# Mixture-of-experts decoder step: the down projection of an expert's first token block multiplied one expert later

## What is computed

```python
def swiglu(x, w_gate, w_up, w_down):
    return (jax.nn.silu(x @ w_gate) * (x @ w_up)) @ w_down
...
        xb = x_pad[tok]
        yb = swiglu(xb, w_gate[e], w_up[e], w_down[e]) * w[:, None]
        return acc.at[tok].add(yb), None
```

## Time and profile before

| | |
|---|---|
| Median of 3 runs | 1901.25 us (1900.89 to 1901.89) |
| Profiled execution, its own time | 1903.72 us |
| Span of its instructions | 1901.9 us |
| Mean granted clock of TensorE in it | 0.962 |
| TensorE busy over the span | 1716.1 us (90%) |
| VectorE, ScalarE, GpSimd busy | 968.8, 779.8, 513.7 us |

### The profile page before, as it was taken

The page is one execution under the profiler, slowest core; times in us unless marked ns, Lnnn a source line. Parts: engine busy times, 40 slices in busy tenths (PEclk is TensorE's granted clock), DMA queues, the critical chain, the costliest instruction groups (busy, mean ns, idle before and its releaser), DMA issues. The chain is left out here.

```text
span 1901.9 us, 25091 instructions
## 1 busy us (share of the span) xinstructions
PE 1716.1 (90%) x7154; PEld 1075.3 (57%) x7155; DVE 968.8 (51%) x1639; ACT 779.8 (41%) x1453; POOL 513.7 (27%) x733
## 2 busy tenths in 40 slices
PE   6999999978985699999999998999999999937998
PEld 4666666545774456556656655656665565623443
DVE  3333333314996354555444545445555544637885
ACT  2222222212331355665555555545556554721221
POOL 0000110000665332333332334223333322411221
PEclk9999999987998799999999998999999999978999
DMA  9200000021111787888777768767787776958650
GB/s 360 100 0 0 0 0 0 15 96 47 67 67 62 255 294 257 274 286 292 255 243 248 257 232 299 246 228 271 260 280 274 260 253 222 337 219 331 270 166 28
DMA packets 124013, 363.70 MB, mean 191 GB/s; under 512 B 28966, under 2 KB 44262, under 8 KB 121389
## 3 DMA queue, kind: packets, MB, share of 16 engines
q1 hardware_dynamic: 87909, 290.85, 44.2%
q0 software_dynamic: 35760, 72.49, 10.7%
q10 hardware_dynamic: 320, 0.07, 0.0%
HBM read 334.52 MB, written 71.91 MB: 214 GB/s over the span
## 5 line engine op out<-in xcount | busy, mean ns | idle before, releaser
L1409 PE MATMUL Y<-raw_d,hT 128*128 128x512 f32 (+1 forms) x768 | 352.1, 602 | 19.7 <-ACT hT L1469 19.7
L197 DVE TENSOR_TENSOR lo_gu<-raw_g,hi_gu 128x1024 fp32r<-128x1024 f32 x130 | 153.5, 1221 | 366.5 <-ACT hi_gu L190 321.3
L1367 PE MATMUL GU<-hi_gu,x_hi 128*128 128x512 f32 (+1 forms) x768 | 322.0, 419 | 5.7 <-issue 4.1
L1367 PE MATMUL GU<-hi_gu,x_lo 128*128 128x512 f32 (+1 forms) x768 | 304.6, 397 | 0.0
L1367 PE MATMUL GU<-lo_gu,x_hi 128*128 128x512 f32 (+1 forms) x768 | 304.3, 396 | 0.0
L1477 ACT ACTIVATE y<-Y,w_t 128x512 f32<-128x512 f32 (+1 forms) x256 | 168.3, 683 | 238.5 <-PE Y L1409 230.6
L1328 POOL DMA_INDIRECT y_dram<-y,to_row x128 | 131.3, 1026 | 472.0 <-ACT y L1477 354.0
L1409 PEld LDWEIGHTS Y<-raw_d,hT 128*128 128x128 f32 (+1 forms) x768 | 132.3, 179 | 178.7 <-issue 167.3
L1317 POOL DMA_INDIRECT rows<-rows_dram,from_row x131 | 159.0, 1214 | 109.1 <-POOL from_row L1315 76.8
L1367 PEld LDWEIGHTS GU<-hi_gu,x_hi 128*128 128x128 f32 (+1 forms) x768 | 136.8, 178 | 77.4 <-issue 39.6
L107 POOL TENSOR_SCALAR st<-st 128x1 f32<-128x1 f32 (+3 forms) x45 | 14.4, 321 | 582.5 <-ACT junk L585 201.0
(11 more groups left out here) (221 smaller groups left out, 2139.3 us busy)
## 6 DMA issues: line engine op xcount, KB each, us to landing
raw_g<-in_w_exp_gate SPq DMA_DIRECT2D x130, 512.0 KB, 5.9
raw_u<-in_w_exp_up SPq DMA_DIRECT2D x130, 512.0 KB, 6.2
raw_d<-in_w_exp_down SPq DMA_DIRECT2D x130, 512.0 KB, 4.9
yk<-y_dram SPq DMA_DIRECT2D x16, 2048.0 KB, 12.7
rows_dram<-row SPq DMA_DIRECT2D x9, 512.0 KB, 2.7
h_dram<-resid SPq DMA_DIRECT2D x9, 512.0 KB, 2.7
w_big<-in_w_in SPq DMA_DIRECT2D x2, 2048.0 KB, 12.8
w_out<-in_w_out SPq DMA_DIRECT2D x1, 4096.0 KB, 18.1
```

The source lines that it names most:

```text
L197: dve.tensor_tensor(part_of(keep, "lo", m, par, h), part_of(keep, "raw", m, par, h), part_of(keep, "hi", m, par, h).bitcast(F32), ALU.subt ...
L1367: ins = pe.matmul(out, lhs[x], rhs[w], start=first and i == 0, stop=last and i == 2)
L1409: ins = pe.matmul(Y[half][0:n, :], hT[b][:, f, :], raw_d[par][:, f, cols], start=f == 0, stop=f == FC - 1)
```

## The change

On TensorE `down(0, ...)` of an expert no longer stands in its own turn but in that of the next expert, with the other `raw_d` buffer (`1 - par`) and a second `hT` buffer. In `one_block` its half 0 stands between the transposes and `h_transposes(0)`, half 1 after that. In `two_blocks` the first matmul of half 0 stands before `h_transposes(0)`, the second between `gate_up(1)` and `h_transposes(1)`, half 1 where it was; `down(1, ...)` stays with its own expert. The first turn multiplies zeros, and one `down(0, ...)` with its copies and its scatter follows the loop. The tables `to_t`, `idx_t` and `w_t` have a column more in front, so that block 0 finds the entry of the expert before.

On SP `load` asks for `gate` and `up` of the next expert (`following`) as before, and last for `down` of this turn's expert `e`, when the first of the counts of the turn before is there. TensorE waits for it before half 1. The first `down` weights are no longer loaded at the start of the router but at the start of the expert stage, where SP waits for them.

```diff
@@ -142,9 +142,9 @@
-                    to_t=mid("to_t", [P, 2, PAIRS + 2], I32),
-                    idx_t=mid("idx_t", [P, 2, PAIRS + 2], I32),
-                    w_t=mid("w_t", [P, 2, PAIRS]),
+                    to_t=mid("to_t", [P, 2, PAIRS + 3], I32),
+                    idx_t=mid("idx_t", [P, 2, PAIRS + 3], I32),
+                    w_t=mid("w_t", [P, 2, PAIRS + 1]),
@@ -915,8 +915,6 @@ (router, SP)
-            for h in range(2):
-                sp.dma_start(part_of(keep, "raw", "d", 0, h), expert_weights(a, "d", 0, h)).then_inc(keep[f"d_ld{h}"], 16)
@@ -1191,7 +1189,9 @@
 
 
             own.did(dve.memset(keep["fill"][:, E:PAIRS], CAP))
-            own.did(dve.memset(keep["to_t"][:, :, PAIRS:PAIRS + 2], Y_ROWS))
+            own.did(dve.memset(keep["to_t"][:, :, 0:1], Y_ROWS))
+            own.did(dve.memset(keep["to_t"][:, :, PAIRS + 1:PAIRS + 3], Y_ROWS))
+            own.did(dve.memset(keep["w_t"][:, :, 0:1], 0.0))
             dve.wait_ge(count_done, TILES + 1)
             own.did(dve.tensor_copy(count[:], C[0:1, 0:E]))
             own.wait()
@@ -1205,11 +1205,11 @@
             own.did(dve.tensor_scalar(rounds[:], top[:, 1:2], 1.0, None, ALU.add))
             dve.wait_ge(tab_ld, 32)
             for b in range(2):
-                own.did(dve.tensor_copy(keep["to_t"][:, b, 0:PAIRS], tab[:, b, :, 0]))
+                own.did(dve.tensor_copy(keep["to_t"][:, b, 1:PAIRS + 1], tab[:, b, :, 0]))
             own.wait()
             own.did(dve.tensor_scalar(keep["idx_t"][:], keep["to_t"][:], 3, None, ALU.logical_shift_right))
             for b in range(2):
-                own.did(dve.tensor_copy(keep["w_t"][:, b, :], tab[:, b, :, 1]))
+                own.did(dve.tensor_copy(keep["w_t"][:, b, 1:PAIRS + 1], tab[:, b, :, 1]))
             own.wait()
 
 
@@ -1229,7 +1229,7 @@
         hi_gu, lo_gu, raw_d = (keep[n] for n in ("hi_gu", "lo_gu", "raw_d"))
         x_hi = [sb(f"x_hi{b}", [P, KC, BLK[b]], F32R) for b in range(2)]
         x_lo = [sb(f"x_lo{b}", [P, KC, BLK[b]], F32R) for b in range(2)]
-        hT = [sb(f"hT{b}", [P, FC, BLK[b]]) for b in range(2)]
+        hT = [[sb(f"hT0{i}", [P, FC, P]) for i in range(2)], [sb("hT1", [P, FC, BLK[1]])] * 2]
         rows = [sb(f"rows{b}", [P, D]) for b in range(2)]
         y = [sb(f"y{b}", [P, D]) for b in range(2)]
         sig = [sb(f"sig{b}", [P, FE]) for b in range(2)]
@@ -1271,17 +1271,17 @@
                              (ple[0:NS, SAMPLE, :], a["p_sample"][0].rearrange("b s d -> (b s) d"))):
                 sp.dma_start(dst, src).then_inc(keep["output_ld"], 16)
 
-            def load(e, m, par):
+            def load(e, following, m, par):
 
                 for name in "gu":
                     for h in range(2):
                         sp.wait_ge(lo_set[name], 2 * m + h + 1)
-                        sp.dma_start(part_of(keep, "raw", name, 0, h), expert_weights(a, name, e, h)).then_inc(
+                        sp.dma_start(part_of(keep, "raw", name, 0, h), expert_weights(a, name, following, h)).then_inc(
                             ld[name][h], 16)
 
+                sp.wait_ge(y_done[1], 2 * m + 1)
                 for h in range(2):
-                    sp.wait_ge(y_done[1], 2 * m + 1)
-                    sp.dma_start(part_of(keep, "raw", "d", 1 - par, h), expert_weights(a, "d", e, h)).then_inc(
+                    sp.dma_start(part_of(keep, "raw", "d", par, h), expert_weights(a, "d", e, h)).then_inc(
                         ld["d"][h], 16)
 
             def gate(n):
@@ -1289,16 +1289,20 @@
                 sp.dma_start(keep["w_big"][:, bass.ds(at, GATE_PIECE)], gate_w[:, bass.ds(at, GATE_PIECE)]).then_inc(
                     gate_ld, 16)
 
-            sp.sem_inc(y_done[1], 1)
+            for h in range(2):
+                sp.dma_start(part_of(keep, "raw", "d", 1, h), expert_weights(a, "d", 0, h)).then_inc(ld["d"][h], 16)
+            for h in range(2):
+                sp.wait_ge(ld["d"][h], 16)
+            sp.sem_inc(y_done[1], 2)
             n_rounds = sp.value_load(rounds[0:1, 0:1], min_val=1, max_val=ROUNDS)
             with sp.Fori(0, n_rounds) as r:
                 with sp.Fori(0, E // 2 - 1) as i:
                     for par in range(2):
-                        e = sp.snap(2 * i + par + 1)
-                        load(e, r * E + 2 * i + par, par)
+                        following = sp.snap(2 * i + par + 1)
+                        load(sp.snap(2 * i + par), following, r * E + 2 * i + par, par)
                         gate(2 * i + par)
                 for n in (E - 2, E - 1):
-                    load((n + 1) % E, r * E + n, n % 2)
+                    load(n, (n + 1) % E, r * E + n, n % 2)
                     gate(n)
                 sp.wait_ge(gate_ld, 16 * E * r + 16 * E)
                 sp.sem_inc(sp_passed, 1)
@@ -1312,7 +1316,7 @@
 
             def gather(b, m):
                 n = BLK[b]
-                own.did(pool.tensor_copy(from_row[b][0:n, :], idx_t[0:n, b, bass.ds(m, 1)]))
+                own.did(pool.tensor_copy(from_row[b][0:n, :], idx_t[0:n, b, bass.ds(m + 1, 1)]))
                 own.wait()
                 pool.indirect_dma_start(
                     out=rows[b][0:n, :], out_offset=None, in_=rows_dram[:, :],
@@ -1322,7 +1326,7 @@
             def scatter(b, m):
                 n = BLK[b]
                 pool_after(pool, keep["passed"], y_st[b], 16 * m + 16)
-                own.did(pool.tensor_copy(to_row[b][0:n, :], to_t[0:n, b, bass.ds(m, 1)]))
+                own.did(pool.tensor_copy(to_row[b][0:n, :], to_t[0:n, b, bass.ds(m + b, 1)]))
                 own.wait()
                 pool_after(pool, keep["passed"], y_ev[1], 2 * m + b + 2)
                 pool.indirect_dma_start(
@@ -1355,9 +1359,11 @@
             own.clear()
             each_pair(pool, pair)
             n = pool.value_load(rounds[0:1, 0:1], min_val=1, max_val=ROUNDS)
+            scatter(0, pool.snap(n * E))
+            own.clear()
             for b in range(2):
                 pool_after(pool, keep["passed"], rows_ld[b], n * (16 * E) + (32 if b == 0 else 16))
-                pool_after(pool, keep["passed"], y_st[b], n * (16 * E) + 16)
+                pool_after(pool, keep["passed"], y_st[b], n * (16 * E) + (32 if b == 0 else 16))
 
         @block.tensor
         def _(pe):
@@ -1398,26 +1404,32 @@
                     ins = pe.transpose(GU[b][:, f * n:(f + 1) * n], hid[b][0:n, f * P:(f + 1) * P], ident[0:n, 0:n])
                 ins.then_inc(h_tr[b], 1)
 
-            def down(b, m, par, half, counts):
+            def down(b, m, par, half, counts, fs=range(FC), more=True):
+
                 n = BLK[b]
-                pe.wait_ge(h_ev[b], m + 2)
-                pe.wait_ge(y_ev[half], 2 * m + b + 1)
                 cols = slice(half * 512, (half + 1) * 512)
-                for f in range(FC):
+                if fs[0] == 0:
+                    pe.wait_ge(h_ev[b], m + b + 1)
+                    pe.wait_ge(y_ev[half], 2 * m + b + 1)
+                for f in fs:
                     if b == 0 and half == 0:
                         pe.wait_ge(ld["d"][f], 16 * m + 16)
-                    ins = pe.matmul(Y[half][0:n, :], hT[b][:, f, :], raw_d[par][:, f, cols], start=f == 0, stop=f == FC - 1)
-                ins.then_inc(y_done[half], counts)
+                    if b == 0 and half == 1 and more:
+                        pe.wait_ge(ld["d"][f], 16 * m + 32)
+                    ins = pe.matmul(Y[half][0:n, :], hT[b][par][:, f, :], raw_d[par][:, f, cols], start=f == 0, stop=f == FC - 1)
+                if fs[-1] == FC - 1:
+                    ins.then_inc(y_done[half], counts)
 
             def two_blocks(m, par):
                 gate_up(0, m, par)
                 transposes(1, m)
                 transposes(0, m + 1)
+                down(0, m, 1 - par, 0, 1, (0,))
                 h_transposes(0, m)
                 gate_up(1, m, par)
-                down(0, m, par, 0, 1)
+                down(0, m, 1 - par, 0, 1, (1,))
                 h_transposes(1, m)
-                down(0, m, par, 1, 1)
+                down(0, m, 1 - par, 1, 1)
                 down(1, m, par, 0, 1)
                 down(1, m, par, 1, 1)
 
@@ -1428,9 +1440,9 @@
                 pe.sem_inc(h_tr[1], 1)
                 gate_up(0, m, par)
                 transposes(0, m + 1)
+                down(0, m, 1 - par, 0, 2)
                 h_transposes(0, m)
-                down(0, m, par, 0, 2)
-                down(0, m, par, 1, 2)
+                down(0, m, 1 - par, 1, 2)
 
             def pair(m, par):
                 filled = pe.value_load(keep["fill"][0:1, bass.ds(m, 1)], min_val=0, max_val=SEQ + NS)
@@ -1439,9 +1451,12 @@
                 with pe.If(filled < P + 1):
                     one_block(m, par)
 
-            pe.wait_ge(blank, 3)
+            pe.wait_ge(blank, 4)
             transposes(0, 0)
             each_pair(pe, pair)
+            m = pe.value_load(rounds[0:1, 0:1], min_val=1, max_val=ROUNDS) * E
```

(20 more changed lines are left out.)

## The result

The changed kernel takes 1915.38 us (median of 6 runs, 1910.35 to 1919.16) where the kernel before, on the same chip, takes 1901.07: a ratio of 1.0074, interval 1.0065 to 1.0084. It is slower by 0.7%; the forecast was 1891, faster by 0.5%. The profiled execution took 1915.49 us (span 1913.6), 11.8 more than that of before.

A forecast was written before the change was run, and what follows sets the result against it. TensorE, busy 995 of 1049 us, was taken to bound the expert stage. Terms -45.1 + 22.4 + 10.7 + 3.5 - 2 = -10.5 us took the profiled 1903.72 to 1893.2, as a median 1891; 8-in-10 range 1876 to 1902.

The forecast's parts named there:

- Removed waits: TensorE's waits for hid (25.4 us) and hT (19.7 us) in the expert stage all go: -45.1 us.
- The added wait in two-block turns: TensorE stands before the second block's h_transposes, with only 2 records ahead: 0.70 us per turn, 32 turns, +22.4 us.
- the lower bound: The added two-block wait counted as idle in a busy table, not by starts: 0.54 us per turn, 17.3 us.
- Lead given up by ScalarE and VectorE: In runs of one-block turns these engines' 11.37 us loop lags the faster TensorE, which stops at hid: +10.7 us, at most 15.
- later transfers: Allowance inside the 15 us upper bound on the ScalarE and VectorE lag: 0.2 us more per further one-block turn.
- forecast by group: The prediction's terms split by turn kind and the turn before: -18.9, -17.8, +14.9 and +10.5 us.
- Rival 2: Transfers become the bound in runs of one-block turns, period stays 11.97: gain within 0.2%, about 1900 us; chance 0.17.
- Down weights: SP's down load for this turn's expert lands in 6.0 us, before TensorE needs it at half 1: cost nothing.
- rival 4: Down weights land in 8.8 us or more, so TensorE waits before half 1; 1906 us per microsecond in dense turns; chance 0.03.
- Rival 3: Gathers come late in runs of three or four one-block turns and TensorE's clock falls, 6.4 us each: slower; chance 0.15.
- The drain: A 65th down with copies and scatter after the loop delays the output stage: +3.5 us, between 2.5 and 6.
- The start: First gathered rows share the queues with 2 MB less, so TensorE may start the expert stage sooner: -2 us.

The follow-up runs named there:

- e1: Changed kernel with both matmuls of the late down's half 0 again between gate_up(1) and h_transposes(1) in two-block turns: 1916.09 us, ratio 1.0062 to the kernel before.
- e7: Changed kernel plus second up buffer and two buffers for the first block's gathered rows, that block's gather ahead of the second's: 1913.61 us, ratio 1.0059.
- e6: Kernel before the change, with only a second buffer for the second half of raw_u added: 1901.1 us, ratio 1.0000.
- e11: Kernel before the change, loading only 64 of the 1024 columns of the down weights: 1900.26 us, ratio 0.9996.
- e2: Changed kernel with a second buffer for the second half of raw_u, so SP asks for it earlier: 1896.23 us, ratio 0.9963 to the kernel before.
- e3: Changed kernel loading only a sixteenth of the down weights, still one up buffer: 1889.15 us, ratio 0.9935 to the kernel before.
- e12: Changed kernel plus second up buffer and two first-block row buffers, gather at its old place but for one expert further on: 1888.68 us, ratio 0.9932.

## Why the prediction was wrong

*Removed waits* (-45.1): right, and too small. No wait for `hT` is left; a one-block turn after a two-block turn gives 1.60 us where its two waits had 1.18. Most of the 0.42 more is a matter of reading. The prediction priced the added wait by starts but took the removed ones as the idle time between records, and in these rows a record runs on past the start of the next. This is the turn from 1014.94 before the change, at the transposes ahead of the first wait:

```profile
1020.57 1.03 PE L1377 MATMUL T<-ident,rows 128*128 128x128 f32 x8
```

`h_transposes` starts 1.55 us after them, at 1022.12, and `down` 1.10 after that, at 1023.22. In the changed kernel, where nothing is waited for at these two places, the next matmul starts 0.21 after `h_transposes` and 0.88 after the transposes:

```profile
783.37 0.38 PE L1404 MATMUL GU<-ident,hid 128*128 128x128 f32 x2
783.58 1.88 PE L1419 MATMUL Y<-raw_d,hT 128*128 128x512 f32 x4
...
790.87 1.03 PE L1383 MATMUL T<-ident,rows 128*128 128x128 f32 x8
791.75 1.88 PE L1419 MATMUL Y<-raw_d,hT 128*128 128x512 f32 x4
```

So by starts the two waits took 0.67 + 0.89 = 1.56 us.

*The added wait in two-block turns* (+22.4): right in kind, too large. A two-block turn after another is 0.44 us longer, not 0.70, nor the 0.54 of the lower bound; e1 takes the whole 0.45 away. The new wait itself has the forecast size: the two records and the `h_transposes` behind them start 1.54 us apart where 0.86 would do, 0.68 lost:

```profile
747.00 1.02 PE L1419 MATMUL Y<-raw_d,hT 128*128 128x512 f32 x2
748.54 0.36 PE L1404 MATMUL GU<-ident,hid 84*128 84x84 f32 x2 [0.51 <-DVE hid L1537]
```

But the two records moved ahead cost less than their 0.86. From the start of the second block's transposes to that of the second `gate_up` this turn takes 2.46 us, and 2.01 in the same turn before. So some 0.4 us of room was there before too, though no wait showed it.

*Lead given up by ScalarE and VectorE* (+10.7, at most 15): **this is the step that failed**, and by its size the sign. It followed the loop that these engines make among themselves and no other. In its place stand, by the two groups of turns behind a one-block turn, 10.7 + 27.3 + 2.9 = about 41 us. The loop of these engines itself was sized well: forecast at 11.37; in e7, where the transfers of that run come in time, ScalarE's output copies of two successive one-block turns start 11.26 apart (802.03 and 813.29). What was left out is a second loop, through the one buffer of `raw_u` and the landing of its transfer. The step allowed 0.2 us for "later transfers". Two things came together: VectorE freed the buffer later against TensorE, since its own loop had not become shorter, and the landing rose. In the 16 turns given above, at the head of each run, that is 1.6 us on the mean and 1.2 (from 5.7 to 6.9); between the two transfers shown it is 2.1. The controls e6 and e11 show that the second loop was hidden before, e2 and e3 that cutting it, from either end, brings 19 and 26 us. Of the rest, e12 shows that the first block's gathered rows take some 6 to 7.5. With both transfers cured the two groups of turns together stand at -2.1 against -2.9 forecast, so by this estimate the engines' lag alone is about 11.5. That kernel takes 1888.7, near the 1891 of the forecast, but this is partly luck: its one-block turns gain 12 us more than was forecast by group, its two-block turns lose 3 more, and the first turn, the drain and the start differ too.

The Trainium skill (Perfetto Trace Analysis, Optimization Strategy) says that a gap which repeats through a stretch, on the engine that should be saturated, can mean that memory has no room for the next tile, and names the count of buffers. The trace agrees: with one more buffer of 4 KB per partition TensorE's waits for `hid` fell from 42.0 us to 19.6, and ScalarE's for the up weights from 28.5 to 4.9.

*Rival 2*, the transfers as the bound, had the right place and the wrong measure: it looked at the share and the rate, which hardly move (0.95 and 338 GB/s before, 0.94 and 338 after in the same three turns), and priced a period that stays at 11.97. It was the time of one transfer that counted, and the period went to 12.72. The rule of the Trainium skill that was weighed there (Perfetto Trace Analysis, Engine Utilization: about 435 GB/s for one core) let that rival fall. The trace agrees with the ceiling, 405 GB/s in the stretch from 792 to 798, and the loss came below it.

*Down weights* (0): right. They land in 9.4 us in the densest run, more than the 8.8 at which rival 4 begins, and still TensorE has no wait for them.

*Rival 3*, late gathers and the clock: a part of the loss, some 3 us of clock in the changed kernel; the gathers become the wait only once the up weights are cured.

*The drain* (+3.5): from the last copies of the loop to the output stage 1702.44 - 1688.80 = 13.6 us against 7.4, so +6.3. The copy into `y0` starts after 5.1, as worked out. Then the last `down`, which had waited 2.4 us for a free `Y`, runs at a lower clock (granted 0.72 from 1690 to 1696; its first four records take 2.87 us where four took 1.88), so that the second copy ends 1.2 late, and from the last scatter to the output stage it is 5.2 us, not 3.5.

*The start* (-2): -2.8.

## What to carry to other kernels

When waits are taken out of the busiest engine's loop, write down every other loop that closes through a single buffer, with its transfer's landing time in it, and compare it with the new period, not the old one; a loop that was 1 us too short to be seen takes the gain and more. Landing times are not constants: here they rose by a fifth on the mean at the head of a run, and by about a third for the worst, so try the sum with that much more. And where a wait is priced by the starts of instructions, price the waits that go by starts too. A request that stands behind another engine's result in an in-order queue isn't moved by a second buffer, only by asking for a later item at that place.

## What was not expected of the hardware

The same 512 KB transfer landed in 5.4 us in a turn of the kernel before and in 7.5 in a turn of the changed one, at the same mean rate over three turns of the densest run (338 GB/s in both). What the runs show of the reason is the `down` load: with a sixteenth of its bytes the mean landing around the end of one-block turns falls from 6.5 us to 5.3 (e3), and in the kernel before from 5.8 to 5.2 (e11). So without these bytes the change hardly raises the landing. In the changed kernel it is asked for 0.4 us behind the up load and not 1.6. That this distance makes the difference is likely but not shown, since no run changes it alone. And a slow transfer need cost nothing: in e2 the landing is longer still, 8.2 us at the median in the second buffer, and almost nothing waits for it.
